# One of three gathered token tiles is summed on VectorE with tokens on partitions, the value chunks stand in six buffers

## What is computed

```
def peer_ffn(h, w_q, subkeys, u, v):
    ...
        expert = jnp.take_along_axis(cand_i, top_pos, axis=-1)   # 8 heads x 16 = 128 experts of a token
        gate = jax.nn.softmax(top_s, axis=-1)
        ue = u[expert]
        ve = v[expert]
        act = jax.nn.gelu(jnp.einsum('thkd,td->thk', ue, ht).astype(jnp.float32), approximate=False)
        return jnp.einsum('thk,thkd->td', (gate * act).astype(ht.dtype), ve)
```

## Time and profile before

| | us |
|---|---|
| three runs: median (lowest to highest) | 2903.1 (2899.68 to 2904.68) |
| the profiled execution: its time | 2909.18 |
| the profiled execution: its span in the trace | 2907.4 |
| of it, up to the second product's start | 1797 |
| PE busy in the span | 2806.9 (97%) |
| DVE busy | 1906.2 (66%) |
| POOL busy | 1549.0 (53%) |
| ACT busy | 901.7 (31%) |

### The profile page before, as it was taken

How to read it: one execution, slowest core, us unless ns; L and a number is a source line. 1 busy time by engine, 2 the same in 40 slices (tenths; PEclk the granted TensorE clock), 3 DMA queues, 4 the chain that set the end, 5 groups by cost and what they waited for, 6 DMA issues and landing times.

```text
span 2907.4 us, 44634 instructions
## 1 busy us (share of the span) xinstructions
PE 2806.9 (97%) x16719; PEld 2372.6 (82%) x16719; DVE 1906.2 (66%) x4442; ACT 901.7 (31%) x1750; POOL 1549.0 (53%) x1088
## 2 busy tenths in 40 slices
PE   7999989999999999999999998999999999999998
PEld 6777667999999999899999998666767766767675
DVE  6022363799888999999999743655555555555554
ACT  4223341322222222366666522222222222222222
POOL 1111020455666677755555563866656566666662
PEclk9999989999999999999999999999999999999999
DMA  3100031345777788899999996989999999899996
GB/s 137 44 30 30 23 131 73 102 144 208 264 271 281 262 274 289 293 360 373 379 381 381 369 344 255 338 303 336 332 332 337 334 322 327 314 333 319 324 324 231
DMA packets 300377, 763.51 MB, mean 263 GB/s; under 512 B 21456, under 2 KB 136528, under 8 KB 297424
## 3 DMA queue, kind: packets, MB, share of 16 engines
q0 software_dynamic: 110592, 402.70, 38.3%
q1 hardware_dynamic: 189648, 359.13, 34.7%
HBM read 669.47 MB, written 92.27 MB: 262 GB/s over the span
## 4 chain that ended last, share of the span: by engine, by line
PE 74%; DVE 8%; POOL 3%; DMA 1%; issue 1%; ACT 1%; ACTq 0%; DVEq 0%; POOLq 0%
PE bank L1832 30%; PE bank L1488 26%; PE wide L1852 6%; PE bank L1796 5%; PE bank L1707 3%; PE bank L1724 2%; POOL w_lo L602 1%; DVE u_row L1309 1%; DVE eq L1296 1%; DMA w_raw<-in_u 1%; PE bank L1733 1%; POOL u_row L611 1%; DVE eq L1294 1%; DVE route L1298 1%; POOL v_row L662 1%
## 5 line engine op out<-in xcount | busy, mean ns | idle before, releaser
L662 POOL DMA_INDIRECT v_row<-in_v,ids_t x384 | 381.6, 994 | 391.2 <-PE wide L1852 283.0
L1488 PE MATMUL bank<-h_hi,w_hi 128*128 128x320 f32 (+1 forms) x2400 | 574.3, 321 | 16.2 <-POOL w_lo L602 13.9
L1488 PE MATMUL bank<-h_hi,w_lo 128*128 128x320 f32 (+1 forms) x2400 | 557.1, 313 | 0.0
L1488 PE MATMUL bank<-h_lo,w_hi 128*128 128x320 f32 (+1 forms) x2400 | 557.1, 313 | 0.0
L1405 DVE TENSOR_TENSOR a_lo<-prod,a_hi 128x384 fp32r<-128x384 f32 (+1 forms) x256 | 264.0, 1031 | 445.4 <-ACT a_hi L969 445.2
L602 POOL TENSOR_TENSOR w_lo<-w_raw,w_hi 128x1024 fp32r<-128x1024 f32 x144 | 367.3, 2551 | 337.7 <-ACT w_hi L889 205.2
L1309 DVE CUSTOM_DVE_ANT_0 u_row<-wide,u_row 128x1024 f32<-128x1024 f32 x384 | 450.2, 1220 | 76.5 <-DMA u_row<-in_u_rows,ids 74.4
L611 POOL DMA_INDIRECT u_row<-in_u_rows,ids x384 | 390.7, 1017 | 113.4 <-issue 73.8
L1488 PEld LDWEIGHTS bank<-h_hi,w_hi 128*128 128x128 f32 x2400 | 400.5, 190 | 23.0 <-POOL w_lo L602 15.0
L1832 PE MATMUL bank<-v_hi,a_hi 128*128 128x512 f32 x1272 | 407.6, 402 | 10.4 <-POOL v_lo L651 5.3
L1488 PEld LDWEIGHTS bank<-h_lo,w_hi 128*128 128x128 f32 x2400 | 406.8, 189 | 4.0
(11 more groups left out here) (211 smaller groups left out, 3480.2 us busy)
## 6 DMA issues: line engine op xcount, KB each, us to landing
w_raw<-in_u SPq DMA_DIRECT2D x128, 512.0 KB, 5.4
v_raw<-in_v SPq DMA_DIRECT2D x32, 2048.0 KB, 19.6
act_d<-act_st SPq DMA_DIRECT2D x128, 320.0 KB, 5.3
g_d<-g_st SPq DMA_DIRECT2D x20, 2048.0 KB, 9.4
a_raw<-act_d SPq DMA_DIRECT2D x32, 768.0 KB, 8.1
g_raw<-g_d SPq DMA_DIRECT2D x32, 768.0 KB, 11.8
w_raw<-in_w_q SPq DMA_DIRECT2D x32, 512.0 KB, 3.4
a_raw<-act_d SPq DMA_DIRECT2D x32, 512.0 KB, 10.5
```

The source lines that it names most:

```text
L662: nc.gpsimd.indirect_dma_start(v_row[k % RING][:, :], None, v_rows, bass.IndirectOffsetOnAxis(ids_t[:, t, TW * s + c:TW * s + c + 1], 0)). ...
L1488: ins = pe.matmul(banks[h][:, 0:n], lhs[:, part], rhs[:, k, h * n:(h + 1) * n], start=(k == 0 and lhs is lhs_hi and rhs is h_hi), stop=(k ...
```

## The change

The third gathered tile (tokens 896 to 1023) leaves PE. `gather_d(k)` fetches, for each of its 128 tokens on its own partition, the row of v of the token's k-th expert, into one of two buffers `d_row`. DVE's `add_row(k)` multiplies it by the token's weight and adds it to the tile's sum `yg[2]` in SBUF, 128 x 1024 in one instruction, 128 times. PE keeps two gathered tiles in 64 steps, two in each half, behind j = 2 and j = 6. Number and size of gathers stay: 384 of 512 KB.

`rows_added(n)` spreads the 128 additions over DVE's loop, one in 1.84 products: 8 or 9 in each group, from n = 4 to n = 238. In POOL's loop gather k stands two products ahead of where addition k - 2 stands in DVE's, and it waits for that addition, since it writes its buffer.

The two buffers take 8 KB from `v_raw`, which now has six chunk buffers (`VR`) in place of eight. Chunks are loaded one by one; each waits until the chunk six before it is lowered. For the first group, six are loaded ahead of the stage and two inside it. The order on SP in a group is: unit, unit, four chunks, unit, two chunks, unit, two chunks (a unit is the activation and the gate of four products). The first row gather buffers and the final adds are moved in keeping (`yg`, `FINAL`).

```
+PT = NGT - 1
+STEPS = PT * P // 4
+GROUP_STEPS = STEPS // NG
+VR = 6
+ROW_K0 = PT * P
...
-    at = {0: (5, 7), 1: (0, 2, 4, 7), HALVES - 1: (0, 2, 4)}.get(h, (1, 4, 7))
-    return [(0 if h == 0 else 3 * h - (h == 1)) + k for k, at_j in enumerate(at) if at_j == j]
+    at = {0: (5, 7), HALVES - 1: (0, 3)}.get(h, (2, 6))
+    return [2 * h + k for k, at_j in enumerate(at) if at_j == j]
+
+
+def rows_added(n):
+
+    return min(max((n - 3) * P // (HALVES * GT - 20), 0), P)
...
-            def load_v(g, s):
-
-                if g:
-                    sp.wait_ge(vl_done, GT * (g - 1) + VJ * (s + 1))
-                sp.dma_start(v_raw[:, VJ * s:VJ * s + VJ, :], v[GT * g + VJ * s:GT * g + VJ * s + VJ, :, :]
-                             .rearrange("j p d -> p j d")).then_inc(v_in[s], 16)
+            def load_v(j):
+
+                if j >= VR:
+                    sp.wait_ge(vl_done, j - VR + 1)
+                sp.dma_start(v_raw[:, j % VR, :], v[j, :, :]).then_inc(v_in[j % VR], 16)
...
+            def gather_d(k):
+
+                if k >= 2:
+                    pool.wait_ge(yd_done, k - 1)
+                nc.gpsimd.indirect_dma_start(d_row[k % 2][:, :], None, v_rows,
+                                             bass.IndirectOffsetOnAxis(ids[:, ROW_K0 + k:ROW_K0 + k + 1], 0)
+                                             ).then_inc(d_in[k % 2], 16)
+
...
+                if j < 2:
+                    gather_d(j)
             for h in range(HALVES):
                 for j in range(GT):
                     if h % 2 and h + 1 < HALVES:
...
+                    for k in range(*(min(rows_added(GT * h + j + d) + 2, P) for d in (2, 3))):
+                        gather_d(k)
...
+            def add_row(k):
+
+                dve.wait_ge(d_in[k % 2], 16 * (k // 2 + 1))
+                if k:
+                    dve.wait_ge(yd_done, k)
+                V.scalar_tensor_tensor(out=yg[PT][:, :], in0=d_row[k % 2][:, :],
+                                       scalar=uh[:, ROW_K0 + k:ROW_K0 + k + 1], in1=yg[PT][:, :],
+                                       op0=ALU.mult, op1=ALU.add).then_inc(yd_done, 1)
+
...
+                for k in range(rows_added(n), rows_added(n + 1)):
+                    if k == 0:
+                        dve.wait_ge(uh_gate, 1)
+                        dve.wait_ge(yd_in, 16)
+                    add_row(k)
```

More of the change, by code:

```diff
@@ L248, in build @@
         pick_t = at("pick_t", 95, [P, 2, 4, TW])
-        v_raw = at("v_raw", 154, [P, GT, D])
+        v_raw = at("v_raw", 154, [P, VR, D])
+        d_row = [at(f"d_row{k}", base, [P, D]) for k, base in enumerate((178, 182))]
         a_raw = [at(f"a_raw{s}", 186 + 6 * s, [P, VJ, WA]) for s in range(2)]
@@ L336, in build @@
         ya_done = sem("ya_done")
-        v_in = [sem("v_in0"), sem("v_in1")]
+        v_in = [sem(f"v_in{k}") for k in range(VR)]
+        d_in = [sem("d_in0"), sem("d_in1")]
+        yd_in = sem("yd_in")
+        yd_done = sem("yd_done")
         a_in = [sem("a_in0"), sem("a_in1")]
@@ L389, in v_turned @@
             return ot[:, 2 * g + c, :]
-        FINAL = [DT, DT + 1, *range(TT[0]), DT + 2, *range(TT[0], DT)]
+        FINAL = [DT, DT + 2, *range(TT[0]), DT + 1, *range(TT[0], DT)]
         def normed(k, n):
@@ L542, in _ @@
                 if k in (0, 1):
-                    load_v(0, k)
+                    sp.wait_ge(g_out[k], 16 * PAIRS)
+                    sp.wait_ge(g_out[1 - k], 16 * PAIRS)
+                    for j in range(VR * k // 2, VR * (k + 1) // 2):
+                        load_v(j)
                 elif k in (2, 3):
@@ L561, in _ @@
                 sp.dma_start(y[i][:, :], x1_d[i]).then_inc(y_in, 16)
[L562 to L565, removed]
+            sp.wait_ge(row_used, ROWS)
+            sp.dma_start(yg[PT][:, :], x1_d[DT + PT]).then_inc(yd_in, 16)
+            sp.dma_start(yg[0][:, :], x1_d[DT]).then_inc(ya_in, 16)
+            for j in range(VR, GT):
+                load_v(j)
             for g in range(NG):
+                more = range(GT * (g + 1), GT * (g + 2)) if g + 1 < NG else ()
                 load_unit(4 * g + 2)
-                if g + 1 < NG:
-                    load_v(g + 1, 0)
                 load_unit(4 * g + 3)
-                if g + 1 < NG:
-                    load_v(g + 1, 1)
+                for j in more[:VJ]:
+                    load_v(j)
+                if more:
                     load_unit(4 * g + 4)
+                for j in more[VJ:VR]:
+                    load_v(j)
+                if more:
                     load_unit(4 * g + 5)
+                for j in more[VR:]:
+                    load_v(j)
             sp.wait_ge(vl_done, NK)
-            sp.dma_start(yg[NGT - 1][:, :], x1_d[NT - 1]).then_inc(ya_in, 16)
+            sp.dma_start(yg[1][:, :], x1_d[DT + 1]).then_inc(ya_in, 16)
             sp.dma_start(gain2[:, :], bcast_row(g_final)).then_inc(gain_in, 16)
@@ L648, in lower_v @@
             def lower_v(g, j):
-                pool.wait_ge(vh_done, GT * g + j + 1)
-                nc.gpsimd.tensor_tensor(v_lo[:, j, :], v_raw[:, j, :], v_hi[:, j, :],
+                n = GT * g + j
+                pool.wait_ge(vh_done, n + 1)
+                nc.gpsimd.tensor_tensor(v_lo[:, j, :], v_raw[:, n % VR, :], v_hi[:, j, :],
                                         ALU.subtract).then_inc(vl_done, 1)
@@ L1467, in _ @@
                         add_half(h - 1, q)
-            add_rows(NGT - 1)
+            add_rows(PT - 1)
             dve.wait_ge(gain_in, 48)
@@ L1859, in turn_rows @@
                 pe.wait_ge(row_used, ROWS)
-                for t in range(NGT):
+                for t in range(PT):
                     pe.transpose(wide[:, t * P:(t + 1) * P], idf[:, t * P:(t + 1) * P], ident[:, :])
                 pe.wait_ge(uh_gate, 1)
-                for t in range(NGT):
+                for t in range(PT):
                     ins = pe.transpose(wide[:, HALF + t * P:HALF + (t + 1) * P], uh[:, t * P:(t + 1) * P],
@@ L1882, in _ @@
             begin = 1
-            for t in range(1, NGT + 1):
-                special = TILE_STEPS * t // 6 if t < NGT else NG - 1
+            for t in range(1, PT + 1):
+                special = TILE_STEPS * t // GROUP_STEPS if t < PT else NG - 1
                 with pe.Fori(begin, special) as it:
```

31 lines of the change are left out of this document (15 added, 16 removed).

## The result

| | before | after |
|---|---|---|
| median (lowest to highest) of four runs | 2902.94 (2899.68 to 2904.68) | 3043.76 (3038.87 to 3045.47) |
| the profiled execution: time, span | 2909.18, 2907.4 | 3044.64, 3042.8 |
| PE busy in the span | 2806.9 (97%) | 2772.4 (91%) |

The ratio after / before is 1.0484, 95% interval 1.0466 to 1.0502: slower by 4.8%. The forecast was 3053, with a range of 2950 to 3105.

A forecast was written before the change was run, and what follows sets the result against it. The prediction took PE, 97% busy, to bound the second product. Profiled 2909.2 - 64.6 removed + 179 hand-over waits + 35 clock = 3058.6; as the profiled execution lies 6.1 over the median, it forecast 3053 us, range 2950 to 3105.

The forecast's parts named there:

- Removed: On PE, 32 steps at 1.85 us go, 59.3 us, plus 5.3 us of gather waits in the first group: 64.6.
- full gain: Whole kernel with the steps gone and no new wait: 2844.6 us profiled, 2838 as forecast for the runs.
- Work alone: Second product's stage: DVE's 154 us of additions, POOL's work and the DMAs at 348 GB/s all have room.
- Order: Gathered rows come late through queue order, so PE waits 12.8 us at each of 14 hand-overs, 179 us.
- lateness: Late rows delay DVE's bank adds at hand-overs into three-tile halves; PE waits a mean 8.0 us at 14 places.
- the place worked out: One hand-over from a two-tile into a three-tile half, reckoned step by step: PE waits 8.5 us before added terms.
- carry-over: A late addition at j = 4 of the two-tile half delays prod, ACT's copy and POOL's work by 2.4 us.
- The port: DVE instructions with two SBUF inputs wait while POOL lowers: 2.4 us a hand-over taken, 0.9 to 4.8 possible.
- The clock: PE's clock drops to half behind waits of 5 us and more: 2.5 us each, fourteen times, 35 us.
- Edits with one answer: Single-chunk loads: chunks 6 and 7 come 5 to 7 us late but hidden; nothing taken, up to 3 us a group.
- The rows come in time: Rival: rows land in time and PE stays the bound, 2838 us, or 2880 with port waits; chance 0.10.
- Additions at twice 1.2 us: Rival: DVE's additions take double, 2.4 us more at 14 places, 3087 us, inside the range; no chance of its own.

The follow-up runs named there:

- the last kernel: Changed kernel with four row buffers, four chunk buffers in the changed kernel's load order, and DVE's bank adds at the head of their loop pass: 2855.1 us, ratio 0.9826.
- the move of the bank adds: DVE's bank adds put at the head of their loop pass: kernel before 2906.7 us, changed kernel 3006.96, changed kernel with four row buffers 2855.1.
- four buffers: Changed kernel with four buffers for gathered rows, not two, and four chunk buffers, not six, chunks loaded in the changed kernel's order: 2905.15 us, ratio 1.0001.
- the kernel with the additions moved: Changed kernel, additions placed away from the hand-over into the three-tile half, gathers one product earlier in POOL's queue, chunks 6 and 7 earlier: 2932.05 us, ratio 1.0095.

## Why the prediction was right, point by point

**Removed.** The 32 steps and the two waits of the first group. With the third tile left out the time was 2857.9, where the forecast of full gain was 2838. The last group, without additions, ran without a wait, as forecast.

**Work alone.** "Room enough" holds: with additions in it PE is busy 893 of 900 us in the last kernel, at 349 GB/s, near the 348 worked out.

**Order.** Right in its cause and in its sum, and the largest term. Forecast: 12.8 us at each of 14 hand-overs, 179 in all. Measured: 10.45 to 14.22, 169 in all, and 4.12 at the fifteenth, which I had left out since the additions were over: their lateness wasn't. Its three parts were less well hit. At the place worked out:

| from PE's start of the two-tile half | forecast | measured |
|---|---|---|
| gather for the first addition starts | 17.75, + 2.4 carried over | 24.0 |
| gather for the second starts | 23.8, + 2.4 | 29.8 |
| from gather to addition | 8.4 | 6.6 |
| hold at the port | 2.4 | 2.3 (3.59 less 1.28) |
| PE's wait | 13.3 | 12.55 |

The carry-over was some 6 us, not 2.4: the addition at j = 4 ran at 11.9, not 9.2, and its effect went through ACT to POOL. The two rows ahead of the banks came quicker than the 8.4 taken, and the two errors cancel for the most part. That is luck of this place: over all 70 additions that waited for their row the median from the gather's start is 8.2 us.

From one hand-over to another the reckoning failed. It gave, with 4.8 for carry-over and port, 10.0 us to the four with one addition ahead of the banks, 13.3 to five with two, the worked place among them, 15.1 to the other four. The measured means are 12.9 (into groups 4, 7, 10, 13), 11.7 (2, 5, 8, 11, 14) and 11.5 (3, 6, 9, 12): the order is the reverse. Where one addition stands behind the end of the half, at j = 1, another stands at j = 7 of the two-tile half, and the reckoning left it out. Into group 4 PE's half ended at 2103.58, and this addition ran 4.2 us later:

```profile
2107.77 1.28 DVE L1476 SCALAR_TENSOR_TENSOR yg<-d_row,uh,yg 128x1024 f32<-128x1024 f32 x1 [12.64 <-DMA d_row<-in_v,ids]
...
2115.32 2.47 DVE L1451 TENSOR_TENSOR y<-y,bank 128x512 f32<-128x512 f32 x4
```

So it is into groups 1, 4, 7 and 10, with waits of 13.07 to 14.22 us; into group 13 the addition at j = 7 ran 7.6 us ahead of PE's end, and the wait is 11.05. The mean of 8.0 for lateness came out near the truth because places priced too low and too high cancel: the sum was better than its terms.

**The port.** Its bounds were 0.9 and 4.8, 2.4 taken, 34 us in all. The runs with no late row, yet with additions, stand 31 us above the kernel without them (2888.8 less 2857.9). That looks like the 34 and isn't the same: 17 of the 31 are longer waits for the banks (41.4 less 24.7), and 15 are the clock behind seven of them, which the forecast counted elsewhere. In after itself the port's share of the waits isn't isolated. And it isn't only the addition that is held; a_lo and prod are, ahead of the same banks, up to 7.75 us.

**The clock.** 2.5 us a wait was forecast, 35 in all. All fourteen show 13.93 to 15.20 us for the three products behind the wait, mean 14.48, so 2.0 over 12.51: 28 us. The term was mis-sized by a fifth. The fifteenth wait, of 4.12 us, cost 2.8 (15.29): there the granted clock still stood at 0.51 from 3 to 6 us behind the wait, where the fourteen had 0.55 to 1.00. Why is open.

**Edits with one answer.** "I take nothing, and up to 3 us a group if not" was right for after, where ACT waits 18.5 us for chunks in all. It is right only because the rows were later still: once they are not, chunks cost 13 us, and two of them moved behind the last unit cost 172. What I failed to name is the step behind j = 7: its place covered bank adds that come a little late, and without it PE waits 24.7 us at 15 hand-overs with no addition in the queue.

**The sum by medians**, each line a run:

| | us | more than the line above |
|---|---|---|
| full gain, as worked out | 2838 | |
| third tile left out | 2857.9 | 20: the banks uncovered, a_lo and prod held |
| additions that wait for nothing, chunks early | 2888.8 | 31: additions and gathers ahead of the banks |
| chunks in their place | 2901.9 | 13: chunks late |
| after | 3043.8 | 142: rows late |

Forecast for the last line were lateness, carry-over and clock, 112 + 34 + 35 = 181, and for the three above it 34 for the port: 215, where it is 206. From ratios to the kernel before in each set instead of medians the four lines are 17, 32, 9 and 148. PE's own account of after agrees: 177 us of waits for the banks and 30 of cold clock make 207. What divides the 31 us between the additions and a_lo is open; the move of the bank adds takes both away at once. So is the spread of some kernels with additions (2843 to 2870 in the last one, 2895 to 2917 with four buffers), twice that of the kernel before beside them (2901 to 2913, 2902 to 2911).

**What was to show it.** PE's waits in place and size, DVE's in the two-tile halves, a clock of half behind each, 287 GB/s where below 300 was said: all there. The period was given too short, near 75 for 77.7; the terms themselves, 63.3 + 12.8 + 2.5, make 78.6.

**The rivals.** "The rows come in time" is what the four buffers make true, and it gives 2905, not 2838 to 2880: the banks' place in the queue is a condition of its own. "Additions at twice 1.2 us": their mean is 1.476 us, median 1.283, longest 4.047, so it is the port, not the operation.

## What to carry to other kernels

Here place in the queue decided, not share: put what frees a resource of the busiest engine ahead of everything that can be held by a transfer or a port, and then look which waits are still on the path. With such work out of its way the kernel stood 159 us of late chunks; with a wait ahead of it, 393 us of late rows cost 142. A buffer ring's lead must cover the producer's own waits besides its landing time, and a number that sizes a ring may also set an order: a change of one should leave the other alone.

## What the runs showed of the hardware

The port works both ways and over several instructions. In the four-buffer kernel a_lo started at 2413.35, 0.27 us ahead of POOL's two lowerings at 2413.62, and lasted 5.40 us where 0.55 is usual; they took 4.71, undisturbed. The prod of 7.75 us started 0.25 ahead of three lowerings of 7.08. In after the lowering at 2403.87 took 3.40 us, where others take 2.35 to 2.40: DVE's addition had started at 2403.73 and ran its usual 1.28. The Trainium skill (SBUF — State Buffer, section Who interferes with whom) gives the pair of ports to whoever issues first, for the whole instruction. The long lowering agrees with it. The a_lo and the prod that came first by the records and still lost do not, nor does the addition at 2419.38, 0.15 us ahead of a lowering and held to 3.59, unless their access began later than their record.

The granted clock fell to 0.50, the 1.2 GHz level, behind each long wait, and was at 1.00 again 6 us later. A wait of 10 to 14 us cost 1.4 to 2.7 us by it, one of 4.12 us 2.8: the price is one for each long wait and doesn't grow with it. Short ones differ: in the kernel with the additions moved, three products behind waits of 2.98 us took 12.53 at one place (2098.49) and 15.28 at another (2511.09).
